# A causal mask moved from the logits into the scan of stick-breaking attention, with projection parts stored in another layout and by another engine

## The reference, cut to what matters

```
def sb_block(q_blk, q_start, k, v, bias):
    """A[t,s] = sigmoid(z_ts) * prod_{s<j<t} (1 - sigmoid(z_tj)), strictly causal."""
    ...
    valid = k_pos[None, :] < q_pos[:, None]
    z = jnp.einsum('bqhd,bkhd->bhqk', q_blk, k) + bias[None, :, None, None]
    lneg = jnp.where(valid, jax.nn.log_sigmoid(-z), 0.0)
    suffix = lax.cumsum(lneg, axis=3, reverse=True) - lneg
    w = jnp.where(valid, jnp.exp(jax.nn.log_sigmoid(z) + suffix), 0.0)
    return jnp.einsum('bhqk,bkhd->bqhd', w, v)
```

## Time and profile before

| what | value |
|---|---|
| median of 3 runs | 3365.73 us (3361.44 to 3368.91) |
| profiled execution | 3368.11 us, its span 3366.5 us |
| TensorE busy | 3155.3 us (94%), mean granted clock 0.969 |
| VectorE busy | 1661.5 us (49%) |
| ScalarE busy | 1399.5 us (42%) |
| GpSimd busy | 889.0 us (26%) |
| DMA | 489.74 MB, mean 145 GB/s |

### The profile page before, as it was taken

How to read it: one execution, slowest core, us unless ns; L and a number is a source line. 1 busy time by engine, 2 the same in 40 slices (tenths; PEclk the granted TensorE clock), 3 DMA queues, 4 the chain that set the end, 5 groups by cost and what they waited for, 6 DMA issues and landing times. The chain is left out here.

```text
span 3366.5 us, 49760 instructions
## 1 busy us (share of the span) xinstructions
PE 3155.3 (94%) x17836; PEld 2474.9 (74%) x17836; DVE 1661.5 (49%) x1967; ACT 1399.5 (42%) x2332; POOL 889.0 (26%) x936
## 2 busy tenths in 40 slices
PE   6999999799799799999999499999999999799998
PEld 6999999556588699999999355555555555466665
DVE  5111122387544411222222388998899897443442
ACT  5111111265311211112211278888888787344442
POOL 0000000254111000000000266776677675100000
PEclk8999999799899899999999699999999999899999
DMA  4122111455255421444431555343433410999995
GB/s 152 62 71 76 69 57 58 159 187 182 103 183 178 147 76 51 176 170 147 165 101 57 137 151 142 79 123 107 119 88 103 123 36 16 354 325 374 366 339 210
DMA packets 257393, 489.74 MB, mean 145 GB/s; under 512 B 27133, under 2 KB 142562, under 8 KB 245922
## 3 DMA queue, kind: packets, MB, share of 16 engines
q1 hardware_dynamic: 232450, 350.61, 32.3%
q0 software_dynamic: 24752, 136.63, 11.3%
HBM read 329.58 MB, written 157.59 MB: 145 GB/s over the span
## 5 line engine op out<-in xcount | busy, mean ns | idle before, releaser
L1736 POOL TENSOR_TENSOR att_w<-att_w,att_rest 128x1023 f32<-128x1023 f32 (+7 forms) x384 | 615.4, 1606 | 303.0 <-DVE att_rest L1703 289.9
L470 PE MATMUL projb_acc<-projb_x_hi,projb_w_hi 128*128 128x416 f32 x1280 | 451.0, 352 | 16.5 <-DVE projb_w_lo L452 16.5
L470 PE MATMUL projb_acc<-projb_x_hi,projb_w_lo 128*128 128x416 f32 x1280 | 449.2, 351 | 0.0
L470 PE MATMUL projb_acc<-projb_x_lo,projb_w_hi 128*128 128x416 f32 x1280 | 448.9, 351 | 0.0
L1564 PEld LDWEIGHTS att_wT_acc<-const_ident,att_w 128*128 128x128 f32 x2176 | 236.9, 142 | 210.2 <-issue 152.9
L1653 ACT ACTIVATE att_rest<-att_z,att_bias 128x1024 f32<-128x1024 f32 (+7 forms) x384 | 333.3, 868 | 85.4 <-PE att_z L1610 55.5
L1703 DVE TENSOR_TENSOR_SCAN att_rest<-att_rest,att_zero 128x128 f32<-128x128 f32 (+7 forms) x256 | 355.0, 1402 | 23.2 <-ACT att_rest L1653 23.1
L292 PE MATMUL proja_acc<-proja_x_hi,proja_w_hi 128*128 128x416 f32 x1000 | 353.7, 354 | 0.8 <-DVE proja_x_lo L265 0.7
L292 PE MATMUL proja_acc<-proja_x_hi,proja_w_lo 128*128 128x416 f32 x1000 | 351.8, 352 | 0.0
L292 PE MATMUL proja_acc<-proja_x_lo,proja_w_hi 128*128 128x416 f32 x1000 | 350.0, 350 | 0.0
L1564 PE MATMUL att_wT_acc<-const_ident,att_w 128*128 128x128 f32 x2176 | 314.9, 281 | 31.2 <-ACT att_k_tok L1668 14.8
(11 more groups left out here) (256 smaller groups left out, 4910.4 us busy)
## 6 DMA issues: line engine op xcount, KB each, us to landing
smp_k_pages<-in_cache_k SPq DMA_DIRECT2D x128, 512.0 KB, 7.2
smp_v_pages<-in_cache_v SPq DMA_DIRECT2D x128, 512.0 KB, 7.2
proj_b<-projb_out POOLq DMA_DIRECT2D x32, 1040.0 KB, 4.4
proj_a<-proja_out POOLq DMA_DIRECT2D x24, 1040.0 KB, 4.5
kq_hi<-early_area POOLq DMA_DIRECT2D x16, 1024.0 KB, 6.0
kq_lo<-early_area POOLq DMA_DIRECT2D x16, 1024.0 KB, 8.9
att_q_hi<-kq_hi SPq DMA_DIRECT2D x60, 256.0 KB, 4.1
att_q_lo<-kq_lo SPq DMA_DIRECT2D x60, 256.0 KB, 5.1
```

What stands on the lines that cost most here:

```text
L470: mm = pe.matmul(acc[:, q, 0:size], w[:, b, k, :], x[:, k, at:at + size], start=(k == 0 and w is w_hi and x is x_hi), stop=(k == KD - 1 an ...
L1736: pool.tensor_tensor(these, these, passed[:, 1:size], ALU.mult).then_inc(w_made, 1)
```

## The change

Five things change. Line numbers of the kernel after are lower by 9 to 34 in the parts concerned.

1. The mask matmul and `diag_mask` go. A PSUM bank `begin` (bf16) is zero but for a 128x128 identity in its last columns. The scan of a masked item adds this instead of zeros and starts from 0 instead of 1: state = state * rest + begin, so that the state is 0 above the diagonal and 1 on it. A carried item adds one zero column of the same bank.
2. `project` stores the parts as `k_parts` and `q_parts`, laid out by pair and span of 512, in four DMAs of 64 partitions for each block (rows of 2 KB) instead of two of 128 (rows of 8 KB). Attention then loads q in one DMA for each part and k in one DMA for each span, or for a whole pair (rows of 4 KB instead of 2 KB or less). The small first pieces of q and k are no longer loaded apart.
3. ScalarE issues all stores of both projections, in its own stream; GpSimd has nothing left to do there.
4. In `att` the turns of pair 0 stand at beats 6, 8, 10 and 12, and a product with v waits for its own turn instead of the last one of the pair.
5. ScalarE loads its table of functions ahead of its first wait in `proja` and `outa`; in `gla` the 3 MB of early weights are issued behind `gate_weights(1)`.

```diff
@@ normalise_project
+            act.preload_act_table_set("sqrt_and_others")
             act.wait_ge(eps_set, 1)
...
+                if gate:
+                    act.wait_ge(gate_made, (n - first_gate) * n_spans + n_spans)
+                else:
+                    act.wait_ge(copied, n * n_spans + n_spans)
+                act.wait_ge(gain_in, 32)
+                act.dma_start(dst[ds(n * P, width), :], out[0:width, b, :]).then_inc(stored[b], 16)
...
-        @block.gpsimd
-        def _(pool):
-            def store(n, i, b, width, gate, follows_gate):
...
-                pool.dma_start(dst[ds(n * P, width), :], out[0:width, b, :]).then_inc(stored[b], 16)
@@ project
+                act.dma_start(dst[ds(jb * P + row, P), :], out[:, b, :]).then_inc(stored[b], 16)
+                if kind == "parts":
+                    act.wait_ge(high_made, no * n_spans + n_spans)
+                    act.wait_ge(low_made, no * n_spans + n_spans)
+                    to = parts[j].rearrange("a u e p h n -> e h p (a u) n")
+                    for part, made in enumerate((high, low)):
+                        for h in range(2):
+                            act.dma_start(to[part, h, :, ds(jb * NCH, NCH), :],
+                                          made(0, SEQ).bitcast(F32)[h * HD:(h + 1) * HD, :].rearrange("p (u n) -> p u n", n=BANK)
+                                          ).then_inc(parts_stored, 16)
...
-                    pool.dma_start(parts[0][ds(no * P, P), :], high(0, SEQ).bitcast(F32)).then_inc(parts_stored, 16)
-                    pool.dma_start(parts[1][ds(no * P, P), :], low(0, SEQ).bitcast(F32)).then_inc(parts_stored, 16)
@@ gla
-            early.load(sp)
             sp.wait_ge(logit_cp, 5)
             gate_weights(1)
+            early.load(sp)
@@ attention_schedule
-            put(7 + m if pair == 0 else 40 * (pair - 1) + LAG + 1 + 2 * m, ("turn", pair, m))
+            put(6 + 2 * m if pair == 0 else 40 * (pair - 1) + LAG + 1 + 2 * m, ("turn", pair, m))
@@ prompt_attention, SyncE
             def load_k(pair):
-                for u in range(NCH):
-                    load_k_span(pair, u, 0, 4, in_k[pair % 2])
...
+                sp.dma_start(k2[:, pair % 2, :, :, :], k_parts[pair].rearrange("u e p h n -> (e p) u (h n)")
+                             ).then_inc(in_k[pair % 2], 16)
...
             def load_q(pair, g):
                 for part, dst in enumerate((q_hi, q_lo)):
-                    for half in range(2):
-                        sp.dma_start(dst[half * HD:(half + 1) * HD, g, :, :],
...
+                    sp.dma_start(dst[:, g, :, :], q_parts[pair, g, part].rearrange("p h n -> p (h n)").unsqueeze(0)
+                                 .broadcast_to([2, HD, 2 * BANK])).then_inc(in_q[g], 16)
@@ prompt_attention, TensorE
-                if j == 4 * g + 3:
-                    pe.wait_ge(copied[1], turn_end[pair])
+                if j % 4 == 3:
+                    pe.wait_ge(copied[1], ring_no["turn", pair, j // 4] + 1)
...
-                if not carried:
-                    pe.matmul(z_ps[:, n % 2, size - P:size], c.ident_bf[:, :], c.diag_mask[:, :], start=True,
-                              stop=False, skip_group_check=True)
...
+            pe.wait_ge(begin_cleared, 1)
+            pe.transpose(begin[:, 1024 - P:1024], c.ident_bf[:, :], c.ident_bf[:, :]).then_inc(begin_made, 1)
@@ prompt_attention, VectorE
-                    dve.tensor_tensor_scan(passing, passing, zero[:, 0:1].broadcast_to([P, size]),
-                                           carry_of(t, h) if carried else rest[:, n % n_rest, 1024:1025],
-                                           ALU.mult, ALU.add).then_inc(scanned, 1)
...
+                        dve.tensor_tensor_scan(passing, passing, begin[:, 0:1].broadcast_to([P, size]),
+                                               carry_of(t, h), ALU.mult, ALU.add).then_inc(scanned, 1)
+                    else:
+                        dve.tensor_tensor_scan(passing, passing, begin[:, 1024 - size:1024][:, ::-1],
+                                               rest[:, n % n_rest, 1024:1025], ALU.mult, ALU.add).then_inc(scanned, 1)
```

More of the change, by code:

```diff
@@ L115, in _ @@
         def _(pool):
-            for t in (c.ident, c.ident_bf, c.diag_mask):
+            for t in (c.ident, c.ident_bf):
                 pool.memset(t[:, :], 0.0).then_inc(zeroed, 1)
-            pool.wait_ge(zeroed, 3)
+            pool.wait_ge(zeroed, 2)
             for t in (c.ident, c.ident_bf):
@@ L231, in evict @@
                                    ACT.Sigmoid if gate else ACT.Copy).then_inc(copied, 1)
+                if gate:
[4 more added lines that the diff above has]
+                act.dma_start(dst[ds(n * P, width), :], out[0:width, b, :]).then_inc(stored[b], 16)
             evict(0, 0, 0, P, False, False)
             over_blocks(act, evict)
+            act.wait_ge(stored[0], 16 * (blocks // 2 + 1))
+            act.wait_ge(stored[1], 16 * (blocks // 2))
         @block.vector
@@ L420, in step @@
                         if q == 0 and from_tile(no, 1):
-                            act.wait_ge(parts_stored, no * 32)
+                            act.wait_ge(parts_stored, no * 64)
                         act.activation(high(at, size), acc[:, q, 0:size], ACT.Copy).then_inc(high_made, 1)
+                if kind == "gate":
+                    act.wait_ge(gate_made, no * n_spans + n_spans)
+                else:
+                    act.wait_ge(copied, n * n_spans + n_spans)
+                act.wait_ge(gain_in, 16 * len(jobs))
+                _, _, _, dst, row = jobs[j]
+                act.dma_start(dst[ds(jb * P + row, P), :], out[:, b, :]).then_inc(stored[b], 16)
[8 more added lines that the diff above has]
+                                          ).then_inc(parts_stored, 16)
             over_blocks(act, step)
+            act.wait_ge(stored[0], 16 * (n_blocks // 2))
+            act.wait_ge(stored[1], 16 * (n_blocks // 2))
+            act.wait_ge(parts_stored, 64 * n_parts)
         @block.vector
@@ L1383, in prompt_attention @@
     k_rows, v_rows, g_rows = 0, D, 3 * D
-    k_parts, q_parts = 0, D
+    k_parts, q_parts = parts
     order = attention_schedule()
@@ L1728, in _ @@
                     n, size = z_no[(kind, pair, *x)], hi - lo
-                    passed = rest[:, n % n_rest, 1024 - size:1024]
+                    passed = rest[:, n % n_rest, 1024 - size:1025]
+                    n_passed = size - 1 if carried else size
                     pool.wait_ge(sig_made, n + 1)
@@ L1734, in _ @@
                     pool.wait_ge(scanned, n + 1)
-                    these = weight(pair, phase, h, t, 0, size - 1)
-                    pool.tensor_tensor(these, these, passed[:, 1:size], ALU.mult).then_inc(w_made, 1)
+                    these = weight(pair, phase, h, t, 0, n_passed)
+                    pool.tensor_tensor(these, these, passed[:, 1:n_passed + 1], ALU.mult).then_inc(w_made, 1)
                     if lo:
```

93 lines of the change are left out of this document (31 added, 62 removed).

## The result

The changed kernel takes 3410.95 us (median of 4 runs, 3406.77 to 3415.55), the kernel before 3364.62 (4 runs, 3361.44 to 3368.91): ratio 1.0137, 95% interval 1.0117 to 1.0157. The change costs 46 us where a gain of 57 was forecast.

What follows compares the result with a forecast made beforehand. TensorE was taken to bound most steady phases of attention (VectorE "below"), transfers its start. Savings of 24 + 19 + 5.3 + 2.9 + 2.5 + 3.3 = 57.0 us from 3368.1 gave 3311.1, hence 3309 as median; 8-in-10 range 3292 to 3330.

Steps and rivals of the forecast that it cites:

- layout and loads: Start of attention, pair 0: larger loads at 369 GB/s, with the spread turns, save 19 us, between 5 and 26.
- the case on the other side: Attention's masked scans get slower with the new operand: 3436 us at half as much again, near 3615 doubled; chance 0.05.
- mask: Attention: 240 mask matmuls at 0.11 us of TensorE's queue each go, taken as 24 us saved, between 0 and 28.
- stores' ends: Ends of both projections: stores by ScalarE save 5.3 us behind projb and 2.9 behind proja, bounds 0 and 9.
- tables: ScalarE's table loads on the way to the first turn: one moves into a wait, one goes; 2.5 us saved, bounds 1 and 3.
- gate weights: gla: TensorE's wait for head 1's gate weights goes, 3.3 us saved, bounds 0 and 4.
- 1.8 in 'first': Steady pair's phase first of attention: removing its 16 masks at 0.11 us each saves 1.8 us of the pair's 3.5.
- the first rival: Attention: something else fills TensorE's gap; the mask is worth 12 us if only "first" shortens (3321), else 3333; chance 0.12.
- two of the three waits should go: Pair 0's phase below: of ScalarE's three waits for the k_tok store, 16.7 us in all, 10 us go.
- the second rival: Start of attention only moves its waits: layout, loads and turns give 5 us instead of 19, total 3323; chance 0.10.
- my own case: Start of attention: layout, loads and turns save 19 us; likeliest total, all parts as summed, 3309 us, chance 0.65.
- the ends keep their length: Projections' ends: another issuing engine saves only about half a microsecond each, sum 7 us smaller, total 3316; chance 0.08.

Runs made afterwards that it cites:

- q_halves_mask_matmul: q_halves with the mask put back as a matmul and the masked scan adding 0: 3341.19 us.
- before_act_stores: The kernel before with only both projections' stores issued by ScalarE in place of GpSimd: 3358.43 us, ratio 0.9978.
- before_tables: The kernel before with only ScalarE's square-root table loaded ahead of the first wait in two stages: 3364.5 us, ratio 0.9998.
- before_gla_order: The kernel before with only gla's early loads for the next stage moved behind head 1's gate weights: 3362.02 us, ratio 0.9986.
- q_halves: The changed kernel with each q load as two DMAs, one per half of the partitions, in place of one with a leading broadcast of 2: 3326.79 us.
- before_q_bcast: The kernel before with each q load as two DMAs by head with a leading broadcast of 2, in place of two by half of the partitions: 3485.92 us.

## Why the prediction was wrong

**The step that failed** is the layout and loads: "While rows of 4 KB are read later in the program the engines move 369 GB/s ... At 369, 1.57 MB take 4.3 us". I priced the new q loads by their packet size alone, on 16 engines. They have packets of 4 KB, and run at 51 to 53 GB/s. The step gave 19 us of gain; with the loads as written, attention lost 65 in the trace, and that one form of access pattern costs 84 us (3410.95 against 3326.79). No rival of mine held this: the case on the other side was the slower scan, which the unchanged 1403 ns refute.

The Trainium skill ("DMA: Bandwidth & Descriptors", section Rules for kernel authors) says it outright: the engines of a DMA are set by the slowest dimension of its access patterns, so "a leading zero-stride broadcast of c copies" keeps it to at most c engines. The traces agree: with the broadcast two packets are under way at a time, at a share of 0.13 and 52 GB/s, against a share of 0.86 and 218 GB/s for the same loads by halves. That the leading size of 2 does it, and not the source that is read twice, is the page's statement: every slow kernel here has both, and no run parts them. The prediction used this page for another rule, and did not hold the new source's outermost dimension against this one.

The other steps, by what the runs gave:

| term | forecast | measured | by |
|---|---|---|---|
| mask | 24 | 14 (13.9 in attention's trace, 14.4 timed) | q_halves_mask_matmul |
| layout, loads, turns, without the broadcast | 19 | 9 | attention 979.7 against 988.5 |
| stores' ends | 8.2 | 7.4 (4.4 to 10.8) | before_act_stores |
| tables | 2.5 | 0.7 (-2.7 to 4.4) | before_tables |
| gate weights | 3.3 | 4.7 (1.3 to 8.1) | before_gla_order |
| sum | 57 | 36; q_halves: 38 (33 to 44) | |
| broadcast on two engines | 0 | -84 | q_halves |

The mask's mechanism was right, and so were the 0.11 us behind turning matmuls; what failed is their count: I took all 16 masks of "first" at that price ("1.8 in 'first'"). Half of them stand behind the products with v, where a mask cost 0.02, and what the first beats gained went into waits. In a steady pair first, middle, above and rest became 0.7, 0.7, 0.4 and 0.2 us shorter: 2.0 instead of 3.3. In size this is close to the first rival ("something else fills TensorE's gap"), which put it at 12, but not in its picture: there only "first" was to shorten.

In the start of attention, by halves, the first scan comes 11.1 us after SyncE's first issue, where it was 7.5 (I said 0.5 later); phase first takes 23.4 us, as forecast (23); phase below takes 40.2, not 33. The step "two of the three waits should go" failed: the waits for `k_tok` were 16.7 and are 15.0 us, with the turns at their old beats 11.7, and when the store is put first, the loads behind it are late instead. That was the second rival ("only moves its waits"), which put the part at 5 instead of 19: with 9 measured, it is nearer than my own case.

The ends of the stages went as forecast: 5.30 us behind projb (5.6) and 3.56 behind proja (3.5). ScalarE's issues in the loops cost nothing, as said (738.5 us for 738.8 in projb). The rival that "the ends keep their length" falls for this kernel: with ScalarE as issuer 5.6 us go at projb's end alone. The landing is about the same (4.2 us in q_halves for 4.4), so what went is time behind it; that it is GpSimd's own was only inferred.

## What to carry to other kernels

Before a rate is put on a new DMA, look at the outermost dimension of both access patterns, not only at the packet: a broadcast written in front costs the load its engines, and what it costs is paid by everything queued behind it. When an instruction is taken from a busy engine, read its price at each kind of place where it stands (0.11 and 0.02 us here), and count nothing where a wait follows that can take the gain. And where the DMA share is at 1.0, don't count on a new order of the transfers: here three orders made other ones late, and gained 4.6 us in the trace at most.

## What the runs showed of the hardware

A q DMA of the broadcast form moves 51 to 53 GB/s, with two packets under way at a time. The next issue on SyncE behind two of them lasts 8 to 10 us (7.99, 9.75), for 0.3 to 0.8 in the kernel before: a slow transfer blocks the engine that issues, not only its own data. By halves, with the DMA engines full, two issues last 3.4 and 5.5 us too.

A 128x128 bf16 matmul in TensorE's stream cost 0.11 us behind turning matmuls of 128 columns and 0.02 behind products with v of 512 columns (q_halves_mask_matmul against q_halves).

TensorE's granted clock fell in the steady state when the loads held it up. In before_q_bcast it waited 6.5 us in pair 2's below (29.2 - 22.7); in middle behind it the clock is 0.89 where it was 1.00 (a part of the stretch at the lower of its two levels, 1.2 GHz for 2.4), and the busy time 26.68 us where it was 24.08. So 4.0 us of waiting cost 2.2 us more in the phase after.

The gla stage differs between executions of the same work. In the five traces with the old order of its loads it takes 256.1 to 262.7 us, at granted clocks of 0.90 to 0.92.
